# Moving a small exponential and its power series out of the first norm of a two-block transformer kernel

## The reference

```python
def rmsnorm(x, g):
    xf = x.astype(jnp.float32)
    y = xf * lax.rsqrt(jnp.mean(xf * xf, axis=-1, keepdims=True) + RMS_EPS)
    return (y * g.astype(jnp.float32)).astype(x.dtype)
...
h = h + mla_mixer(rmsnorm(h, a_norm_g[j]), ...)      # latent attention, 8 heads
h = h + rglru_mixer(rmsnorm(h, b_norm_g[j]), ...)    # gated linear recurrence
...
log_a = -LRU_C * r.astype(jnp.float32) * jax.nn.softplus(-lam.astype(jnp.float32))
a = jnp.exp(log_a)
```

## Time and profile before

| | |
|---|---|
| time, median of 3 runs | 815.59 us (815.41 to 815.99) |
| profiled execution, first to last instruction | 814.4 us |
| TensorE busy | 801.8 us, 98% |
| weight loads of TensorE | 747.8 us, 92% |
| VectorE busy | 602.5 us, 74% |
| ScalarE busy | 550.7 us, 68% |
| TensorE clock, mean granted | 0.998 |
| HBM | 135.83 MB read, 168 GB/s |

### The profile page before, as it was taken

The page is one execution under the profiler, slowest core; times in us unless marked ns, Lnnn a source line. Parts: engine busy times, 40 slices in busy tenths (PEclk is TensorE's granted clock), DMA queues, the critical chain, the costliest instruction groups (busy, mean ns, idle before and its releaser), DMA issues.

```text
span 814.4 us, 14821 instructions
## 1 busy us (share of the span) xinstructions
PE 801.8 (98%) x5854; PEld 747.8 (92%) x5854; DVE 602.5 (74%) x1140; ACT 550.7 (68%) x1045; POOL 0.2 (0%) x4
## 2 busy tenths in 40 slices
PE   8999999999999999999999999999999999999997
PEld 8989899999999899988989999998899888888886
DVE  7999997989987995876657475866757667564664
ACT  7876876699977888767455465668866756553652
POOL 0000000000000000000000000000000000000000
PEclk9999999999999999999999999999999999999999
DMA  9533344665564544464837365444434657554451
GB/s 329 191 103 130 105 147 144 201 201 169 182 202 130 175 137 130 155 226 137 281 117 248 130 238 178 130 133 153 149 111 157 211 177 236 188 175 167 166 181 52
DMA packets 40676, 137.83 MB, mean 169 GB/s; under 512 B 4640, under 2 KB 6176, under 8 KB 40608
## 3 DMA queue, kind: packets, MB, share of 16 engines
q1 hardware_dynamic: 39600, 135.70, 50.0%
q10 hardware_dynamic: 1008, 1.20, 0.4%
HBM read 135.83 MB, written 1.05 MB: 168 GB/s over the span
## 4 chain that ended last, share of the span: by engine, by line
PE 88%; DVE 9%; ACT 1%; issue 1%; DMA 1%; ACTq 0%; DVEq 0%
PE bank L796 15%; PE bank L803 15%; PE bank L798 14%; PE bank L797 14%; PE bank L804 7%; PE bank L807 5%; PE bank L809 5%; PE bank L808 5%; DVE weights_lo L1753 2%; PE bank L1171 2%; DVE temp L1753 1%; DMA weights_raw<-stream_dram 1%; DVE arena L1753 1%; DVE operand L1753 1%; DVE temp L1756 1%
## 5 line engine op out<-in xcount | busy, mean ns | idle before, releaser
L1753 DVE TENSOR_TENSOR weights_lo<-weights_raw,weights_hi 128x1024 fp32r<-128x1024 f32 (+3 forms) x257 | 299.7, 1191 | 37.1 <-ACT weights_hi L1249 36.7
L796 PE MATMUL bank<-operand,weights_hi 128*128 128x256 f32 (+1 forms) x1092 | 313.5, 287 | 1.6 <-DVE weights_lo L1753 1.0
L798 PE MATMUL bank<-operand,weights_lo 128*128 128x256 f32 (+1 forms) x1092 | 309.5, 283 | 0.0
L797 PE MATMUL bank<-operand,weights_hi 128*128 128x256 f32 (+1 forms) x1092 | 309.1, 283 | 0.0
L1249 ACT ACTIVATE weights_hi<-weights_raw 128x1024 fp32r<-128x1024 f32 (+3 forms) x257 | 257.3, 1031 | 76.2 <-PE bank L798 34.6
L796 PEld LDWEIGHTS bank<-operand,weights_hi 128*128 128x128 f32 x1092 | 206.1, 189 | 7.6 <-issue 5.0
L798 PEld LDWEIGHTS bank<-operand,weights_lo 128*128 128x128 f32 x1092 | 206.2, 189 | 0.0
L797 PEld LDWEIGHTS bank<-operand,weights_hi 128*128 128x128 f32 x1092 | 205.8, 188 | 0.0
L803 PE MATMUL bank<-operand,weights_hi 128*128 128x512 f32 x512 | 180.1, 394 | 0.0
L804 PE MATMUL bank<-operand,weights_lo 128*128 128x256 f32 x512 | 143.6, 281 | 0.0
L803 PEld LDWEIGHTS bank<-operand,weights_hi 128*128 128x128 f32 x512 | 96.2, 188 | 21.3
(11 more groups left out here) (212 smaller groups left out, 791.8 us busy)
## 6 DMA issues: line engine op xcount, KB each, us to landing
weights_raw<-stream_dram SPq DMA_DIRECT2D x242, 512.0 KB, 4.3
weights_raw<-stream_dram SPq DMA_DIRECT2D x6, 384.0 KB, 3.5
temp<-memT_dram SPq DMA_DIRECT2D x8, 256.0 KB, 5.2
weights_raw<-stream_dram SPq DMA_DIRECT2D x6, 256.0 KB, 5.7
residual<-xT_dram SPq DMA_DIRECT2D x6, 136.0 KB, 5.5
constants<-consts_dram SPq DMA_DIRECT2D x1, 536.5 KB, 6.9
arena<-consts_dram SPq DMA_DIRECT2D x1, 512.0 KB, 4.3
out_dram<-arena SPq DMA_DIRECT2D x2, 256.0 KB, 2.5
```

Of the source, the lines that this page charges most:

```text
L796: e.matmul(to, w_h, x_h, start=start, stop=False, skip_group_check=True)
L797: e.matmul(to, w_h, x_l, start=False, stop=False, skip_group_check=True)
L798: return e.matmul(to, w_l, x_h, start=False, stop=stop, skip_group_check=True)
L1753: return e.tensor_tensor(to, a, b, op)
```

## The change

The steps get other numbers in the table, and the dummy instruction gets another function. ScalarE's `small` goes from 8.5 to 17.45, directly ahead of `lambda_exp`. VectorE's parts 1, 2 and 3 go from 8.25, 8.5 and 9.2 to 32.45, 34.4 and 35.4.

```diff
@@ TIMES
-    ("scalar", "small"): (8.5,),
+    ("scalar", "small"): (17.45,),
     ("scalar", "lambda_exp"): (17.5,),
@@ TIMES
-    ("vector", "small"): (4.5, 8.25, 8.5, 9.2, 40.2, 15.83),
+    ("vector", "small"): (4.5, 32.45, 34.4, 35.4, 40.2, 15.83),
@@ scalar, before the first weights
                 if i == 1:
                     act.wait_ge("eps")
-                    copy(cols[:, 21:22], EPS_COL, scale=1.0)
+                    e.activation(cols[:, 21:22], EPS_COL, ACT.Sqrt, bias=0.0, scale=1.0)
```

## The result

The changed kernel takes 818.26 us (median of 10 runs, 817.02 to 819.64), the kernel before 815.92 us (10 runs, 815.41 to 816.72). The ratio is 1.0027, with a 95% interval of 1.0019 to 1.0035: slower by 2.3 us, or nearly 0.3%.

A forecast was written before the change was run, and what follows sets the result against it. TensorE was taken to bound the kernel, with 88% of the chain of waits. The terms -1.57 + 0.34 + 0.04 + 2.6 = +1.4 us, added to 815.6, gave 817.0 us; range 814.4 to 818.6.

The forecast's parts named there:

- rival C: Behind norm b: the 2.6 us stall sends TensorE's clock to the lower level, +2.5 us, 819.5 us; chance 0.06.
- rival A: Before 50 us: something VectorE's lateness hid holds TensorE, norm a's gain isn't kept, +2.9, 818.5 us; chance 0.16.
- What bounds norm a: Norm a: TensorE waits for VectorE's series, not ScalarE's root; moving the series away gains 1.57 us.
- The table load, under 0.1 us: Norm a: the 1.28 us load ahead of ScalarE's root is booked at under 0.1 us on the path.
- ScalarE's 0.34 us at 17.45: Between the splits of units 17 and 18: ScalarE's two small instructions are on the path, +0.34 us.
- Part 1 at nothing: At 32.45: part 1's 1.03 us fits VectorE's 0.99 us wait for TensorE, costing at most 0.04 us.
- Parts 2 and 3, +2.6: Norm b: both parts, put ahead of the reciprocal, make TensorE wait +2.6 us, not given back.
- Rival B: Norm b: the wait doesn't arise because VectorE has time in hand, -1.23, 814.4 us; chance 0.12.
- The sum, +1.4: Whole kernel: -1.57 + 0.34 + 0.04 + 2.6 = +1.4 us, giving 817.0 us, 0.17% slower.

The follow-up runs named there:

- e7: The changed kernel measured again, with nothing altered: 819.50 us, five runs.
- e11: The changed kernel measured a third time, as control for e10 in the same session: 820.43 us, four runs.
- e1: The kernel before with only ScalarE's dummy made a square root; exponential and series stay in norm a: 816.07 us, ratio 1.0002.
- e2: The changed kernel with the old copy as ScalarE's dummy: five runs, three from 817.31 to 817.62 and two at 819.44 and 820.08 us.
- e5: e4 with ScalarE's small exponential at 18.8 instead of 17.45, in its wait for TensorE: 814.88 us, ratio 0.9989 to the kernel before.
- e3: The changed kernel with part 3 of the series at 40.1, behind the reciprocal of norm b: 816.11 us, ratio 1.0002 to the kernel before.
- e4: The changed kernel with parts 2 and 3 behind norm b's reciprocal, at 36.3 and 40.1: 815.33 us, ratio 0.9989 to the kernel before.
- e8: e4 with 19 linked VectorE instructions ahead of the reciprocal of the norm before the second model's first feed-forward layer: 818.17 us.
- e6: The changed kernel with 15 more linked VectorE instructions ahead of part 3, lengthening the stall at norm b: 822.73 us.
- e9: As e8, with 34 linked VectorE instructions instead of 19: 823.27 us.
- e10: The changed kernel with 19 more products on TensorE directly ahead of its wait for norm b's reciprocal: 817.93 us, eight runs.

## Why the prediction was right, and where it was not

**The median lies in the range** (814.4 to 818.6), and the terms of the sum came out nearly as forecast. But 817.0 was 1.3 us low, and "slower by over 0.2%" had been given 0.32, where the medians say 0.29% (the interval of the ratio reaches down to 0.19%). A third of a microsecond of the 1.3 is the starting value, 815.59 from three runs against 815.92 from ten. The rest, 0.9 us, is most likely rival C, which the sum left out and which the traces of e7 and e11 show.

**That the median lies inside is in part luck.** The upper end was rival A's, a gain that is not kept (its own sum gives 818.5), and A did not happen. C was left out of the range. Only five of the ten runs of the changed kernel lie at 818.6 or below, and the medians of the same kernel in e7 and e11, 819.50 and 820.43, lie above it.

- *What bounds norm a.* Right. The stall was VectorE's series: moved away, 1.48 us are gained; e1 shows that the root's place is nothing to it. The forecast of 1.57 put the spread 0.13 us behind the last product, and it comes 0.22 behind, as the earlier trace rows had it. No new wait took the gain in norm a, so rival A is out. One reading was wrong without consequence: the longest of TensorE's other waits is 1.0 us, at line 1239 in the start, and not 0.7.
- *The table load, under 0.1 us.* Mis-sized. e2 measured 0.32 us at the spread and 0.23 at the end. The step took the old root to end at 26.02 and the reciprocal to start at 26.05. On the same clock, counted from the first mean, they came at 26.37 and 26.40 in e2, because ScalarE had waited for loads of weights.
- *ScalarE's 0.34 us at 17.45.* Right, 0.36 in the trace, and e5 takes just that away.
- *Part 1 at nothing.* Right: its last row starts at 133.60 and the tile's addition follows at 133.68, with no wait between, where the earlier trace rows had 0.91.
- *Parts 2 and 3, +2.6.* Right: 2.61 between mean and spread of norm b; e3 and e4 take it away in two steps. The stretch of VectorE grew by 2.88 as worked out (3.0 less 0.1). Rival B is out.
- *The sum, +1.4.* Right for an execution at full clock: +1.45 in the trace, and the lower five runs (median 817.53) lie 1.6 above the kernel before.
- *Rival C at 0.06.* This is the step of the reasoning that failed. "1.41 us of idleness did nothing, and 2.6 is less than twice that" was no reason; the longest idle stretch of the trace bounds nothing above itself. The clock fell in the profiled executions of e7 and e11. By the times, which are no proof for a run without a trace (e1 and e8), it fell in half of the ten first runs and in all nine of the later two measurements. The price was put at 2.5 us, from the start of the program; it was 1.36 us in e7 and 1.49 in e11. The Trainium skill, "TensorE: Matmul & The Clock Gate", part 1, says that idleness brings the slow level back and work lifts it; e6, e9 and e10 agree, with 0.50 granted behind stalls of 5.4 and 5.0 us, and 1.00 where the stall was filled. At 2.5 us the traces go both ways.

Why the same kernel kept the clock in five runs and lost it in the others stays open, as does why it fell in each run of the later sessions. In e8, with 2.24 us of idleness in the profiled execution, it didn't fall there. The stall itself is the same in the profiled executions that kept the clock (2.53 us in the changed kernel, 2.51 in e2) and in those that lost it (2.53 in e7, 2.52 in e11).

## What to carry to other kernels

A wait that is removed by moving work is moved with it, unless the work goes where its engine waits: give each moved piece the idle time that it will fill, by its row, and check what stands behind it in order. Small work that nobody needs soon belongs directly behind the step that others wait for (e4), or into a wait of its engine for TensorE (e5). For TensorE a stall has a second price: when it is longer than any that the trace already holds, take the slow level of the clock behind it as a case with real weight, in the range as well as in the chances. Cheap products put into the stall may buy it back (e10, with one trace and eight runs).

## What was not expected of the hardware

The clock may or may not fall for one and the same stall: 2.5 us of idleness at the same instruction left 1.00 in two profiled executions (the changed kernel and e2) and 0.50 in two (e7 and e11), and in e11 the fall came only 1.5 us behind the start of the spread. The changed kernel's first ten runs form two groups of times 1.8 us apart, 0.2% of the time, which is nearly as much as the change itself; that they are these two cases is likely and not shown. And the start of the program varies by up to 2.35 us between executions (first mean at 22.10 to 24.45 us, the latter in e9, with identical work up to there), so spans of single executions that differ by a microsecond say nothing until they are counted from a common point. In e9 the products still start 0.23 us apart at 12.5 us; in the kernel before they start 0.12 us apart from 6.2 us on. The granted clock in the rows is 1.00 in both, so in the start the spacing of products is the better sign of the two.
